# Expert rows added to x in DRAM by the scattering DMA, in a two-layer attention and mixture-of-experts kernel

## The reference

```python
def hier_moe(h, w_group, b_group, w_expert, b_expert, w_gate, w_up, w_down):
    ...                       # group softmax, top 2 of the 8 experts of one group
    gates = g_w * jax.nn.softmax(top_v, axis=-1)          # 512 x 2 weights
    ...                       # rows sorted by expert, padded to blocks
    def expert_block(args):
        xb, e = args
        return (jax.nn.silu(xb @ w_gate[e]) * (xb @ w_up[e])) @ w_down[e]
    ys = lax.map(expert_block, (xs, block_e)).reshape(rows, h.shape[1])
    return jnp.zeros_like(h).at[row_tok].add(ys * row_w[:, None].astype(h.dtype))

# in each layer, g_f a row of 1024 gates that all tokens share:
x = x + g_f * hier_moe(modulate(rmsnorm(x, ...)), ...)
```

## Time and profile before

| what | us |
|---|---|
| median of 3 runs | 2134.31 |
| lowest and highest of them | 2129.99, 2136.19 |
| the profiled execution, its own time | 2130.43 |
| its span, from the first to the last instruction | 2128.5 |
| PE busy in the span | 1787.7 |
| DVE, ACT, POOL busy | 528.9, 446.7, 116.0 |

### The profile page before, as it was taken

How to read it: one execution, slowest core, us unless ns; L and a number is a source line. 1 busy time by engine, 2 the same in 40 slices (tenths; PEclk the granted TensorE clock), 3 DMA queues, 4 the chain that set the end, 5 groups by cost and what they waited for, 6 DMA issues and landing times.

```text
span 2128.5 us, 17028 instructions
## 1 busy us (share of the span) xinstructions
PE 1787.7 (84%) x6466; PEld 833.1 (39%) x6466; DVE 528.9 (25%) x1145; ACT 446.7 (21%) x1081; POOL 116.0 (5%) x118
## 2 busy tenths in 40 slices
PE   5899988779989999885576999978689989999872
PEld 2455544444433333322233454543544433333321
DVE  1665652331000000000745122224410000000003
ACT  3133442211111111110300143330221211111100
POOL 0000001100001000000000000000000000010000
PEclk9999999779999999998688999987689999999997
DMA  9863532238999999999245021140169999999994
GB/s 360 288 236 119 198 110 92 93 126 301 397 395 388 388 389 389 383 385 381 106 138 187 31 79 40 62 161 19 40 218 350 395 394 388 387 388 380 389 389 190
DMA packets 251863, 539.99 MB, mean 254 GB/s; under 512 B 12804, under 2 KB 50149, under 8 KB 251774
## 3 DMA queue, kind: packets, MB, share of 16 engines
q1 hardware_dynamic: 233536, 501.24, 64.2%
q0 software_dynamic: 17440, 36.77, 4.7%
q10 hardware_dynamic: 798, 0.80, 0.1%
HBM read 537.67 MB, written 28.34 MB: 266 GB/s over the span
## 4 chain that ended last, share of the span: by engine, by line
PE 67%; DMA 22%; DVE 6%; issue 2%; ACT 2%; SPq 1%; POOL 0%; POOLq 0%; DVEq 0%; ACTq 0%
PE psum L1867 23%; DMA ring<-in_moe_w_up_dram 17%; PE psum L1684 8%; PE psum L1501 8%; PE psum L1898 7%; PE psum L1654 4%; DMA ring<-in_ada_w_dram 3%; PE psum L1556 3%; PE psum L1786 1%; PE psum L1849 1%; DVE W L982 1%; PE psum L1802 1%; SPq L423 1%; PE psum L1530 1%; PE psum L1667 1%
## 5 line engine op out<-in xcount | busy, mean ns | idle before, releaser
L1867 PE MATMUL psum<-ring,V 128*64 128x512 f32 (+1 forms) x2048 | 627.2, 629 | 94.3 <-DMA ring<-in_moe_w_up_dram 79.3
L1867 PEld LDWEIGHTS psum<-ring,V 128*64 128x64 f32 (+1 forms) x2048 | 236.0, 162 | 451.8 <-issue 451.5
L1898 PE MATMUL psum<-ring,V 128*64 128x512 f32 (+1 forms) x1024 | 303.8, 596 | 12.8 <-issue 7.9
L871 ACT ACTIVATE V<-psum,modall,scls 128x128 f32<-128x128 f32 x336 | 126.5, 457 | 515.7 <-PE psum L1849 515.7
L1898 PEld LDWEIGHTS psum<-ring,V 128*64 128x64 f32 (+1 forms) x1024 | 106.8, 153 | 154.2 <-issue 154.2
L982 DVE SCALAR_TENSOR_TENSOR W<-ring,cact,W 128x512 f32<-128x512 f32 (+1 forms) x224 | 138.5, 618 | 7.7
L1347 DVE TENSOR_TENSOR V<-V,psum 128x512 f32<-128x512 f32 x42 | 28.9, 689 | 411.0 <-PE psum L1867 411.0
L1501 PE MATMUL psum<-HT,ring 128*128 128x512 f32 x256 | 119.9, 615 | 3.7 <-DMA ring<-in_a_w_qkv_dram 3.7
L1360 DVE COPY HT<-psum 128x512 f32<-128x512 f32 x42 | 29.0, 692 | 314.8 <-PE psum L1898 314.8
L880 ACT ACTIVATE V<-psum 128x512 f32<-128x512 f32 x42 | 25.1, 597 | 376.7 <-PE psum L1867 376.7
L1353 DVE COPY V<-psum 128x512 f32<-128x512 f32 x42 | 29.0, 691 | 287.7 <-PE psum L1878 287.7
(11 more groups left out here) (256 smaller groups left out, 1519.7 us busy)
## 6 DMA issues: line engine op xcount, KB each, us to landing
ring<-in_moe_w_gate_dram SPq DMA_DIRECT2D x64, 2048.0 KB, 21.1
ring<-in_moe_w_up_dram SPq DMA_DIRECT2D x64, 2048.0 KB, 20.0
ring<-in_moe_w_down_dram SPq DMA_DIRECT2D x64, 2048.0 KB, 19.0
ring<-in_ada_w_dram SPq DMA_DIRECT2D x16, 2048.0 KB, 15.2
ring<-in_ada_w_dram SPq DMA_DIRECT2D x16, 1024.0 KB, 5.3
ring<-in_a_w_qkv_dram SPq DMA_DIRECT2D x8, 1024.0 KB, 12.1
ring<-in_kv_ada_w_dram SPq DMA_DIRECT2D x4, 2048.0 KB, 15.4
V<-expert_rows POOLq DMA_DIRECT2D x8, 1024.0 KB, 8.1
```

The source lines that it names most:

```text
L871: ins = act.activation(V[:, 2 * D + b * D + k * P:2 * D + b * D + (k + 1) * P], bank[0][:, q * P:(q + 1) * P], ACT.Identity, bias=mod[:, 2 ...
L1867: ins = pe.matmul(bank[2 + 2 * i + b][half * w:(half + 1) * w, :], V[:, col:col + w], slot3(x)[:, k, :], start=(k == 0), stop=(k == KC - 1))
L1898: ins = pe.matmul(bank[6 + hf][half * w:(half + 1) * w, :], V[:, col:col + w], slot3(x, 4)[:, k, hf * HALF:(hf + 1) * HALF], start=(k == 0 ...
```

## The change

What it does:

- The gate of a row goes with its slot. The routing tables get a second half (`weigh`), so that the eight matmuls give, for each slot of each tile, the token and the gate (`slot_gate`). `dst` is gone, `tok` serves for the scatter too. For half tiles there are two columns of indices (`tok_half`), one with the upper 64 rows out of bounds and one with the lower.
- DVE takes both PSUM banks of a tile itself (`y_out`), and multiplies with the row's gate and with `gf_row` on the way. ACT's copy is gone.
- ACT writes x (2 MB) to a DRAM tensor before the experts: `next_x` in layer 0, the output itself in layer 1.
- The scatter is an indirect DMA that adds to that tensor. Each waits until the one before has landed. A half tile has two, one for each expert, since both may hold a row of the same token. A layer has 32 scatters in place of 21.
- At the end of layer 0 POOL reads `next_x` back into `X` in four chunks of 0.5 MB, and layer 1's norm, on ACT and DVE, stands alone at the head of the layer. At the end of layer 1 nothing is read, combined or written.

```diff
@@ gpsimd
                 def scatter(rows, b, signal):
-                    pool.indirect_dma_start(ys_d[l], bass.IndirectOffsetOnAxis(ap=rows, axis=0),
-                                            HT[:, b * D:(b + 1) * D], None,
-                                            bounds_check=last_row, oob_is_err=False).then_inc(signal, 16)
+                    pool.indirect_dma_start(acc_d[l], bass.IndirectOffsetOnAxis(ap=rows, axis=0),
+                                            HT[:, b * D:(b + 1) * D], None, compute_op=ALU.add,
+                                            bounds_check=last_token, oob_is_err=False).then_inc(signal, 16)
...
                     pool.wait_ge(*s["y_evac"](p * 2 + 2))
-                    scatter(dst[:, column(p)], b, s["scat"][b].sem)
-                for b in range(2):
-                    pool.wait_ge(*s["scat"][b](turns["scat"][b]))
+                    if p == 0:
+                        pool.wait_ge(acc_in, 16 * (l + 1))
+                        pool.wait_ge(*s["half_ready"](1))
+                    for i in range(halves(p)):
+                        if p + i:
+                            pool.wait_ge(*s["scat"](16 * (ROW_DMAS[p] + i)))
+                        scatter(tok_half[:, i, column(p)] if halves(p) == 2 else tok[:, column(p)], b, s["scat"].sem)
+                pool.wait_ge(*s["scat"](16 * ROW_DMAS[NB]))
...
-                for c in range(TC):
-                    if c >= 3:
-                        pool.wait_ge(*s["comb_free"](c - 2))
-                    at = V[:, (c % 3) * 2 * D:(c % 3 + 1) * 2 * D].rearrange("p (k n) -> p k n", k=2)
-                    pool.dma_start(at, ys_d[l].rearrange("(k c p) n -> c p k n", k=2, p=P)[c]).then_inc(rows_in[c], 16)
+                if l == 0:
+                    for c in range(TC):
+                        pool.dma_start(x3[:, c, :], acc_d[0][c * P:(c + 1) * P, :]).then_inc(rows_in[c], 16)
@@ scalar, between the squares and the last root of the norm ahead of the experts
+                act.dma_start(acc_d[l].rearrange("(c p) n -> p c n", p=P), x3).then_inc(acc_in, 16)
                 root(s["arg2"], s["root2"], TC - 1)
@@ vector, routing
-                dve.tensor_tensor(OB, GE[:, :, 0:NB], GE[:, :, 1:NB + 1], ALU.subtract)
+                step(dve.tensor_tensor(OB[:, :, 0:NB], GE[:, :, 0:NB], GE[:, :, 1:NB + 1], ALU.subtract))
+                step(weigh(OB, NB))
+                dve.tensor_tensor(OB[:, :, 0:NB], OB[:, :, 0:NB], ids(NB), ALU.mult)
@@ vector, tiles
-                def y_half(e, b):
-                    dve.wait_ge(*s["dn_pe"](e * 2 + 2))
-                    dve.wait_ge(*s["y_evac"](e * 2 + 1))
-                    if e >= 2:
-                        dve.wait_ge(*s["scat"][b](16 * (e // 2)))
-                    dve.tensor_copy(HT[:, b * D + HALF:(b + 1) * D], bank[7][:, :]).then_inc(s["y_evac"].sem, 1)
+                def y_out(p, b):
+                    if p == 0:
+                        dve.wait_ge(*s["gate_row"](4))
+                    if p >= 2:
+                        dve.wait_ge(*s["scat"](16 * ROW_DMAS[p - 1]))
+                    for hf in range(2):
+                        dve.wait_ge(*s["dn_pe"](p * 2 + hf + 1))
+                        to = slice(b * D + hf * HALF, b * D + (hf + 1) * HALF)
+                        dve.scalar_tensor_tensor(HT[:, to], bank[6 + hf], slot_gate[:, COLS[p]:COLS[p] + 1],
+                                                 gf_row[:, hf * HALF:(hf + 1) * HALF], ALU.mult, ALU.mult).then_inc(s["y_evac"].sem, 1)
@@ vector, end of the layer
-                    step(dve.tensor_scalar(r0, r0, gates[:, 0, c:c + 1], None, ALU.mult))
-                    step(dve.scalar_tensor_tensor(r0, r1, gates[:, 1, c:c + 1], r0, ALU.mult, ALU.add))
-                    step(dve.tensor_tensor(r0, r0, gf_row, ALU.mult))
-                    dve.tensor_tensor(x3[:, c, :], x3[:, c, :], r0, ALU.add).then_inc(s["x_new"].sem, 1)
```

More of the change, by code:

```diff
@@ L80, in moe_order @@
     return order
+ROW_DMAS = [sum(halves(p) for p in range(n)) for n in range(NB + 1)]
 MOE_ORDER = moe_order()
@@ L261, in program @@
         bank = [psum[:, 512 * i:512 * (i + 1)] for i in range(8)]
-        tok_ov, dst_ov = (XN[:, OV_ROUNDS * E * i:OV_ROUNDS * E * (i + 1)].bitcast(I32) for i in range(2))
+        tok_ov, gate_ov = XN[:, 0:OV_ROUNDS * E].bitcast(I32), XN[:, OV_ROUNDS * E:2 * OV_ROUNDS * E]
         ident, flip = C[:, C_ID:C_ID + P], V[:, 5376:5376 + P]
@@ L277, in program @@
         xn_d = [dram(f"xn_scratch{l}", [S, D]) for l in range(LAYERS)]
-        ys_d = [dram(f"expert_rows{l}", [2 * S, D]) for l in range(LAYERS)]
+        acc_d = [dram("next_x", [S, D]), out[0]]
         w_in = [sem(f"w_in{i}") for i in range(RING)]
@@ L595, in _ @@
                             step(pool.tensor_copy(tokc[:, 0:1], tok_ov[:, ds(e + b * E, 1)]))
[L596 removed]
+                            pool.tensor_tensor(pause[:, 0:1], C[:, 0:1], C[:, 1:2], ALU.add)
+                            step(pool.tensor_copy(gatec[:, :], gate_ov[:, ds(e + b * E, 1)]))
+                            pool.tensor_tensor(pause[:, 0:1], C[:, 0:1], C[:, 1:2], ALU.add)
                             gather(tokc[:, 0:1], 0, o["g"].sem)
                             pool.wait_ge(*o["y"](e * 2 + (2 * u0 + 2)))
[L599 to L601 removed]
+                            pool.tensor_tensor(pause[:, 1:2], C[:, 0:1], C[:, 1:2], ALU.add)
+                            scatter(tokc[:, 0:1], 0, o["scat"].sem)
                             pool.wait_ge(*o["scat"](e * 16 + (16 * u0 + 16)))
@@ L604, in _ @@
                     step = main_step
-                pool.sem_inc(s["scat_all"].sem, 1)
-                for c in range(TC):
-                    if c >= 3:
-                        pool.wait_ge(*s["comb_free"](c - 2))
-                    at = V[:, (c % 3) * 2 * D:(c % 3 + 1) * 2 * D].rearrange("p (k n) -> p k n", k=2)
-                    pool.dma_start(at, ys_d[l].rearrange("(k c p) n -> c p k n", k=2, p=P)[c]).then_inc(rows_in[c], 16)
+                if l == 0:
+                    for c in range(TC):
+                        pool.dma_start(x3[:, c, :], acc_d[0][c * P:(c + 1) * P, :]).then_inc(rows_in[c], 16)
         @block.scalar
@@ L1003, in top_of @@
                     return dve.tensor_tensor_reduce(to, scores, table, -1.0, -NEG, ALU.add, ALU.min, to_max)
+                norm(s["ss_ready"], s["rms_arg"], s["rms_root"], s["xn_ready"])
                 if l == 0:
-                    norm(s["ss_ready"], s["rms_arg"], s["rms_root"], s["xn_ready"])
                     for i in range(4):
@@ L1321, in _ @@
                 dve.wait_ge(*s["tab_pe"](1))
-                slot_table(bank[2][:, 0:NB], NB, dst[:, :], tok[:, :], s["tok_ready"].sem, 912)
+                slot_table(bank[2][:, 0:2 * NB], NB, slot_gate[:, :], tok[:, :], s["tok_ready"].sem, 912)
+                dve.wait_ge(*s["tok_ready"](1))
+                for i in range(2):
+                    ins = dve.tensor_scalar(tok_half[:, i, :], tok[:, :], C[:, C_HALF + i:C_HALF + i + 1], None, ALU.add)
+                ins.then_inc(s["half_ready"].sem, 1)
                 dve.wait_ge(*s["tok_ready"](1))
@@ L1922, in _ @@
                         for a in range(2 * TC):
-                            ins = pe.matmul(bank[2][:, 0:E], W[:, 2048 + a * P:2048 + (a + 1) * P], ohs[:, a, :],
+                            ins = pe.matmul(bank[2][:, 0:2 * E], W[:, 2048 + a * P:2048 + (a + 1) * P], ohs[:, a, :],
                                             start=(a == 0), stop=(a == 2 * TC - 1))
```

94 lines of the change are left out of this document (39 added, 55 removed).

## The result

| | median of 7 runs, us | lowest, highest |
|---|---|---|
| before | 2131.27 | 2125.73, 2138.06 |
| changed | 2142.66 | 2139.87, 2147.77 |

The ratio is 1.005, with a 95% interval of 1.0031 to 1.0069. The forecast was 2120, with a range of 2101 to 2148.

The account below looks back on a forecast made before the run. From about 540 us the DMA engines set the loop's pace; each layer's end is a serial chain. Layer ends -22.3 and -13.2, routing +2.0, DMA work +17, waits +2 give -14.5 us from 2134.3: 2120, range 2101 to 2148.

Parts of the forecast that it names:

- The loop's DMA work: In both expert loops, each adding scatter row costs one more read: 17 us lost, ends 0 and 51.
- the sign that the prediction named for this term: In a saturated 50 us of the loop: q0's share 7.8% instead of 5.2%, weights' MB 2 to 4% below 18.40.
- The loop's waits: In the loops, gathers queue on POOL behind a half tile's serial scatters: 2 us lost in all, 0 to 12.
- The early stall: Early in the layer, a gather needed at 575.05 comes late, so PE would stand 5 us once.
- Layer 1's end: After the last copy, two serial adding scatters replace read back, combining and store: 22.3 us gained.
- Layer 0's end: Between layers, four serial adding scatters, then x read back; PE starts at 1024.4 instead of 1037.63: 13.2 us gained.
- Routing: Ahead of the first tile, extra table operations, wider matmuls and issuing x's store: 1.0 us lost a layer, 2.0 in all.
- Nearly free: Rival: adding costs almost nothing in the loop; without the 17 us the sum is -31.5, 2103 us; chance 0.22.
- Dear: Rival: in the loop, adding costs three reads' worth, 51 us instead of 17; sum +19.5, 2154 us; chance 0.18.
- Stalls at each gather: Rival: slow serial landings make gathers late at some eight wide tiles; at 20 us a landing, 2197 us; chance 0.06.

Follow-up runs that it names:

- experiment 5: Changed kernel with only a wide tile's rows laid differently, ranks 32 to 63 in the upper half of the partitions: ratio 0.9927 to the kernel before, loops 1090.6 us.
- experiment 2: Changed kernel with POOL issuing the next gather between a half tile's two scatters: ratio 1.004 to the kernel before, loops 1117.7 us, 3.8 less than the changed kernel.
- experiment 8: Changed kernel with SP instead of POOL waiting for layer 1's last scatters: ratio 1.0035 to the kernel before, last part 13.0 us instead of 16.3.

## Why the prediction was wrong, by its steps

**The loop's DMA work: the step that failed.** The prediction divided the added bytes by all 16 engines: "4.19 x 42.5 / 16 = 11.1 us of all engines", and took three quarters. The price of a row was right in size: 66 instead of 42 us a MB over all indirect DMAs, and 17.6 us in the loops with rows spread, where 17 were forecast. The division by 16 was wrong. The rows lie in a tile's first partitions, so by the count of experiment 5 the busiest engine carries 114 and 115 rows where an even share is 64, and the term measures 35.1 us. Its upper end, 51 us, held, but for a cause that was not named. The DMA share of 1.03, on which the step leaned, is a mean over engines and can't show this. Nor could the sign that the prediction named for this term: q0's share came to 8.8% where it expected 7.8% (for 8% more bytes than before), and the weights to 4.9% less where it expected 2 to 4%. That sign weighs mean work, and came out near its value while the term came to twice its forecast. The prediction also cited the Trainium skill, Collectives: The Full Stack, section "The bandwidth ceiling: the fold count and why AG ≠ RS ≠ AR", which says of ReduceScatter that it is slower by its second read and not by the addition. In size these runs agree, 17.6 us with rows spread against the prediction's estimate of 22 by the full ratio; none of them tells the read from the addition.

**The loop's waits: near in size.** Forecast 2 us; the loops are 4.3 us longer with plain scatters than before, and the early gather gave back 3.8, both not far above the 1.5 us between two executions of the same loops. The early stall came, 4.54 us.

**Layer 1's end: mis-sized, 15.7 instead of 22.3 us.** Landings in the quiet took 4.5 and 4.1 us where 3.5 was chosen for each (1.6 us together). The rest, 5.0 us, is that the last landing was followed by 1.4 us in the sum and by 6.4 in the trace. That row of before ends with POOL's next DMA, which is not the end of the program.

**Layer 0's end: 9.8 instead of 13.2 us.** The four serial landings were right to 1.8 us (POOL reads back 18.6 us after the last matmul; 16.9 forecast). The remaining 1.7 us lies between POOL's read back and PE. The norm's four chunks on ACT now follow each other without a DVE chunk between them, 8.3 us from the first square to PE, and a table load of 1.28 us stands among them, which before fell into a wait of ACT for DVE.

**Routing: within its ends.** The two parts that hold it differ by -0.9 and -1.2 us where +1.0 each was forecast. The start of layer 0's experts lies at 455 to 464 us over these kernels, so one execution doesn't resolve a microsecond here.

**The rivals.** Nearly free: rejected, plain scatters gain 35 us in the loops. Dear: its term came to 35 us and its side of zero was reached, but a row is not dear. Stalls at each gather: rejected by experiment 2.

## What to carry to other kernels

Where the DMA engines set the pace, don't cost an added transfer by the mean of the engines alone: look at which partitions the rows lie in. Spreading rows over the partitions gained 0.8% in the kernel before with no change to the work, and 1.8% in the changed one. Adding in DRAM trades a read back at the end for a read of each row in the loop: here it lost 0.5% with rows packed into the first partitions and won about 0.5% with rows spread, so the layout is to be settled first. And with rows spread, the product with g_f at PSUM and a read back at the end came to the same time (0.9857 against 0.9872), so the adding is not needed for the gain.

## What was not expected of the hardware

Two arrangements of the same rows, with about the same bytes and mean DMA share (1.03 and 1.05) in 50 us of the loop, differ by 17.1 to 17.9 us in a loop of some 550 us. An adding indirect DMA holds POOL for 1.57 us where a plain one takes 0.97. Where the last wait stands on POOL, the program ended 6.4 us after the landing, with plain scatters as with adding ones; with the last store waited for on SP, as before, it was 0.4 us, and 3.2 us in experiment 8, where POOL had issued a scatter shortly before.
